# S5 in chunks of four tokens with three tables made on the chip; conditioning pairs inside norms; weight slabs used up one at a time

## The chip, the core and the metric

The kernel runs on one core of one Trainium2 chip, as one program with one launch. The metric is device time in microseconds (us), from the first to the last instruction and the little that lies around them. Five engines work side by side and meet through semaphores: PE multiplies matrices into PSUM, DVE and ACT work on SBUF and PSUM element by element, POOL on SBUF alone, and SP issues most of the transfers. A profile names an instruction by its line in the source, its engine and the tiles that it writes and reads.

## What is computed

The model is a decoder trunk of two layers. It handles 256 prompt tokens (one sequence) and 64 sample tokens (8 sequences of 8), so 320 tokens in all, with a width of 1024. Everything is float32. Cut to what matters here:

```python
for layer in range(2):
    sh1, sc1, g1, sh2, sc2, g2 = split(silu(c) @ ada_w[layer] + ada_b[layer])
    h = rmsnorm(x) * (1 + sc1) + sh1
    m = hgrn2(h)  if layer == 0 else  s5(h)
    x = x + g1 * m
    h = rmsnorm(x) * (1 + sc2) + sh2
    f = swiglu(h) if layer == 0 else  moe_top2_of_8(h)
    x = x + g2 * f
y = rmsnorm(x)

def s5(h):                                # 64 groups of 16 channels, 64 complex states in each group
    lam = exp(a * dt)                     # complex, one for each state
    bu  = B @ h                           # 16 channels -> 64 complex states, for each token
    xs[t] = lam * xs[t-1] + bu[t]
    y   = real(C @ xs) + d * h
    z   = gelu(y)
    return (z @ wa) * sigmoid(z @ wb), xs[last]
```

## The kernel before, in words

Activations lie with channels on partitions: `xT` and `hT` hold 8 blocks (`kt`) of 128 channels by 320 tokens. Each engine has one program, written out by hand as a list of instructions and waits, so the order on an engine is the order of the source. The stages follow one another: conditioning pairs 0 to 3, norm, HGRN2 input products (`head_in`, L556), scores and states, output product (L764), norm, dense SwiGLU (`gate_up`, L779, then the output product at L803), norm, S5, GLU (L870), norm, router, then eight experts (L931) and a last norm.

**Weights** come through `ring`, four slots of one 1 MB slab. SP runs down a fixed list (`slabs`); `put(n)` at L326 waits until `slab_credit` reaches n + 1 and then issues the load. The semaphore starts at 3, and PE adds to it when it begins to use a slab, for by then the slab before it is used up. In the dense output product PE waits for both halves of a block (two slabs of 704 KB), adds one credit at the first product, and the second half's credit only at the start of the conditioning product that follows (`mod_rows(q, half, 5, 2)`). In `gate_up` and GLU two slabs are likewise credited together.

**Conditioning** is made in 24 pairs of slabs, q = 0 to 23. A pair is two `mod_rows` on PE (L499), a copy by ACT (`mod_copy`, L1055), a `mod_turn` on PE (L512) and a `mod_bias` on DVE. Pairs 4 to 11 lie beside the HGRN2 input products, 12 to 15 in the dense output product, 16 to 23 in the S5 stage.

**A norm** is a Square on ACT (L1037), column sums on PE (L535), a Sqrt on ACT (L1040), and a reciprocal, products and shifts on DVE, which end with `h_ready`.

**S5** goes through 16 windows of two state groups (a state group is 128 partitions: two channel groups of 64 states). `states_in` (L825) multiplies all 320 tokens by the real and the imaginary input matrix, ACT copies the result from PSUM (L1140), `rotate` turns it by the angle of the token (the prompt part on POOL at L1702, the sample part on DVE), DVE runs real scans along the tokens with the magnitude as factor (L1527, L1529), `rotate` turns everything back on DVE (12 operations at L1232), and `states_out` (L836) multiplies by the output matrix. The helper `tt` puts nearly all elementwise products on L1232 (DVE) and L1702 (POOL). Before that, in the HGRN2 input stage, DVE builds the input and output matrices (5120 columns), PE transposes them, POOL stores them to memory (`prep`, 2.6 MB) and SP loads them back (`kept`) after HGRN2 has left the space. The load of the HGRN2 sample state (`st0`) is issued by ACT right after the input products and waits for that store, because it takes the same space.

**After S5** SP writes the final states, waits for that (`s5_out`), and then loads the first five expert slabs; four more wait for the fourth norm. DVE waits for `s5_out` too before it clears the router's tiles.

## Time and profile before

| what | us |
|---|---|
| three runs | 2151.43, 2152.88, 2154.42 |
| median | 2152.88 |
| profiled execution, its own time | 2154.64 |
| its span, from the first to the last instruction | 2152.8 |

Share of the span in which an engine is busy: PE 84%, DVE 54%, ACT 35%, POOL 27%. These are averages over stages that have different limits, so the profile is read stage by stage. The page's line of 40 slices already shows it: PE stands at 9 tenths in most slices and at 4 in slices 15 to 19, and in those DVE stands at 9 and the granted PE clock at 5 tenths. Busy time on PE is modelled (a matrix product in float32 appears as two records, a transposition as one), so distances between starts are safer than busy times.

### The profile page before, as it was taken

How to read it: one execution, taken by the hardware profiler on the slowest of the kernel's cores; microseconds unless marked ns; L12 is line 12 of the kernel's file. 1: busy time of each engine (PE TensorE's matmuls, PEld its weight loads, DVE VectorE, ACT ScalarE, POOL GpSimd, SP SyncE). 2: the span in 40 equal slices, each digit the busy share in tenths (PEclk: the TensorE clock that was granted, in tenths of full speed). 3: DMA queues.
4: the chain of work that ended last, by engine and by line, in shares of the span. 5: the costliest groups of instructions: out<-in, count | busy, mean ns of one | idle time of the engine just before them, and what ended most of it. 6: DMA issues, size and time to landing. Idle time of an engine off the chain costs nothing.

```text
span 2152.8 us, 26882 instructions
## 1 busy us (share of the span) xinstructions
PE 1801.6 (84%) x10335; PEld 1395.8 (65%) x10335; DVE 1152.0 (54%) x1464; ACT 744.9 (35%) x789; POOL 578.7 (27%) x284
## 2 busy tenths in 40 slices
PE   3799998699987754444497899999999999999995
PEld 2568875477755531112175797979888888888793
DVE  4413404300000049999713576767676777778675
ACT  1110020011100011111212575757575757667571
POOL 0000212595000024554300132423233332424140
PEclk7799999899998865555597799999999999999997
DMA  5688121633334421111153498989898988888884
GB/s 178 180 289 268 40 78 40 195 117 117 117 107 138 118 86 57 61 59 59 40 174 124 156 314 293 351 273 338 272 326 291 308 303 298 303 298 301 299 305 141
DMA packets 365803, 420.56 MB, mean 195 GB/s; under 512 B 17948, under 2 KB 339757, under 8 KB 365494
## 3 DMA queue, kind: packets, MB, share of 16 engines
q1 hardware_dynamic: 363542, 413.02, 58.2%
q10 hardware_dynamic: 2064, 4.19, 0.7%
q0 software_dynamic: 144, 2.62, 0.3%
q8 instruction: 35, 0.57, 0.1%
q14 instruction: 18, 0.15, 0.0%
HBM read 410.87 MB, written 8.95 MB: 195 GB/s over the span
## 4 chain that ended last, share of the span: by engine, by line
PE 69%; DVE 19%; issue 4%; DMA 3%; ACT 3%; POOL 1%; SPq 0%; DVEq 0%; ACTq 0%; POOLq 0%
PE PS L931 32%; DVE arena L1232 10%; PE PS L779 9%; PE PS L803 5%; PE PS L917 4%; PE PS L870 3%; PE PS L556 3%; DVE exact L1232 2%; PE PS L673 2%; DVE arena L1527 2%; PE PS L764 2%; PE PS L463 2%; PE PS L535 2%; PE PS L1010 2%; DMA ring<-in_ffn_w_out 1%
## 5 line engine op out<-in xcount | busy, mean ns | idle before, releaser
L931 PE MATMUL PS<-exact 128*112 128x256 f32 (+1 forms) x5280 | 770.5, 305 | 26.1 <-DVE exact L1232 24.0
L931 PEld LDWEIGHTS PS<-exact 128*112 128x112 f32 x5280 | 685.2, 175 | 95.1 <-DVE exact L1232 31.9
L1232 DVE TENSOR_TENSOR exact<-arena,exact 128x2048 fp32r<-128x2048 f32 (+1 forms) x162 | 320.7, 1984 | 128.2 <-ACT exact L1171 126.7
L1171 ACT ACTIVATE exact<-arena 128x2048 fp32r<-128x2048 f32 x162 | 309.7, 1913 | 41.6 <-PE PS L931 41.5
L1702 POOL TENSOR_TENSOR arena<-arena 128x512 f32<-128x512 f32 (+4 forms) x128 | 191.3, 1514 | 448.8 <-ACT arena L1140 398.4
L1702 POOL TENSOR_TENSOR exact<-arena,exact 128x1024 fp32r<-128x1024 f32 x56 | 192.1, 3436 | 258.3 <-ACT exact L1171 258.3
L1232 DVE TENSOR_TENSOR arena<-arena 128x128 f32<-128x128 f32 (+7 forms) x399 | 241.4, 657 | 27.5 <-PE PS L616 14.3
L1232 DVE TENSOR_TENSOR exact<-ring,exact 128x2048 fp32r<-128x2048 f32 (+1 forms) x104 | 229.7, 2215 | 49.0 <-ACT exact L1171 48.1
L1702 POOL TENSOR_TENSOR exact<-ring,exact 128x1024 fp32r<-128x1024 f32 x32 | 104.0, 3249 | 495.2 <-ACT exact L1171 495.2
L1171 ACT ACTIVATE exact<-ring 128x2048 fp32r<-128x2048 f32 x104 | 198.0, 1912 | 20.5 <-PE PS L931 20.5
L779 PE MATMUL PS<-hT,ring 128*128 128x320 f32 x704 | 192.2, 436 | 12.8 <-DVE hT L1256 12.8
L779 PEld LDWEIGHTS PS<-hT,ring 128*128 128x128 f32 x704 | 135.1, 192 | 69.9 <-DVE hT L1256 13.3
L836 PE MATMUL PS<-arena 128*32 128x320 f32 x128 | 37.7, 741 | 144.0 <-DVEq L1532 144.0
L803 PE MATMUL PS<-arena,ring 128*128 128x320 f32 x352 | 116.2, 498 | 31.2 <-DMA ring<-in_ffn_w_out 30.2
L803 PEld LDWEIGHTS PS<-arena,ring 128*128 128x128 f32 x352 | 77.4, 223 | 69.8 <-issue 48.6
L1232 DVE TENSOR_TENSOR arena<-arena,PS 112x256 f32<-112x256 f32 (+2 forms) x162 | 78.6, 490 | 79.1 <-PE PS L651 44.9
L836 PEld LDWEIGHTS PS<-arena 128*32 128x32 f32 x128 | 9.2, 158 | 169.3 <-DVEq L1532 158.3
L556 PE MATMUL PS<-hT,ring 128*128 128x320 f32 x384 | 109.7, 443 | 0.8 <-DMA ring<-in_hgrn_w_in 0.8
L1232 DVE TENSOR_TENSOR arena<-work,PS 128x320 f32 x22 | 10.8, 489 | 182.1 <-PE PS L779 182.1
L1232 DVE TENSOR_TENSOR gtmp<-PS,mod 128x64 f32<-128x64 f32 x16 | 3.6, 225 | 177.5 <-PE PS L803 149.7
L556 PEld LDWEIGHTS PS<-hT,ring 128*128 128x128 f32 x384 | 73.5, 195 | 34.0 <-issue 6.8
L463 PE MATMUL PS<-const,arena 112*128 112x112 f32 (+8 forms) x322 | 56.8, 283 | 42.2 <-DVE xT L1330 21.9
(189 smaller groups left out, 1644.1 us busy)
## 6 DMA issues: line engine op xcount, KB each, us to landing
arena<-in_moe_w_in SPq DMA_DIRECT2D x109, 1024.0 KB, 7.5
ring<-in_moe_w_in SPq DMA_DIRECT2D x75, 1024.0 KB, 9.2
arena<-in_moe_w_out SPq DMA_DIRECT2D x56, 1024.0 KB, 5.1
ring<-in_ada_w SPq DMA_DIRECT2D x48, 1024.0 KB, 6.5
ring<-in_moe_w_out SPq DMA_DIRECT2D x33, 1024.0 KB, 7.3
ring<-in_ffn_w_in SPq DMA_DIRECT2D x22, 1024.0 KB, 6.3
ring<-in_hgrn_w_in SPq DMA_DIRECT2D x16, 1024.0 KB, 8.0
ring<-in_ffn_w_out SPq DMA_DIRECT2D x16, 704.0 KB, 4.6
```

Of the source, the lines that this page charges most:

```text
L463: return pe.transpose(out, in_, ident[0:k, 0:k])
L535: last = pe.matmul(PS[:, 7, 0:T], const[:, C_ONE:C_ONE + P], hT[:, k, :], start=(k == 0), stop=(k == KT - 1))
L556: last = pe.matmul(PS[:, bank, 0:T], ring[:, n % RING, k * 256 + (h % 2) * P:k * 256 + (h % 2) * P + P], hT[:, k, :], start=(k == 0), stop ...
L779: last = pe.matmul(PS[:, 2 * (t % 2) + m, 0:T], ring[:, (n + m) % RING, k * 256 + sub * P:k * 256 + sub * P + P], hT[:, k, :], start=(k == ...
L803: last = pe.matmul(PS[:, dt % 2, 0:T], ring[:, (n + k // 11) % RING, (k % 11) * P:(k % 11 + 1) * P], mid[:, k, :], start=(k == 0), stop=(k ...
L836: last = pe.matmul(PS[q:q + 32, 4 + k % 2, 0:T], cct[a][:, k, q:q + 32], vb[w % 2][a][:, j, :], start=(a == 0), stop=(a == 1), skip_group_ ...
L870: last = pe.matmul(PS[:, 2 * sub + m, 0:T], ring[:, (n + m) % RING, k * 256 + sub * P:k * 256 + sub * P + P], hT[:, k, :], start=(k == 0), ...
L917: last = pe.matmul(PS[:, 6 + half, k * P:k * P + CAP], htok[0:TOK[i], i, kk * P:(kk + 1) * P], pick[0:TOK[i], i, :], start=(i == 0), stop= ...
L931: last = pe.matmul(out, a[x], w[y], start=first and m == 0, stop=end and m == 2)
L1171: A(wparts[0][:, j % HRING, :], eslab(j), ACT.Copy).then_inc(sem("rounded"), 1)
L1232: return V.tensor_tensor(out, a, b, op)
L1702: return G.tensor_tensor(out, a, b, op)
```

## The change

**S5** works on chunks of four tokens: 80 chunks (64 of the prompt, two for each sample). PE transposes `hT` for each token of the chunk (`tokens_out`, 4 transpositions for each block), DVE copies, PE transposes again (`chunks_in`, 4 transpositions) so that (token in chunk, channel) lies on partitions, ACT copies to `u2`. One table `Zm` takes the 64 inputs of a chunk to the state that the chunk adds (`states_in`: 16 products of 64 by 64 by 80 for each block). Angles are turned and scanned over 64 chunks only (`turn_and_scan`, four times: three operations of 128x512, two scans of 512 and six operations of 128x504 on DVE, and three of 128x512 on POOL for the other half of the first rotation); samples need no scan, POOL makes their two chunks with ten operations of 128x64. The table `Tm` takes the chunk's inputs to its own outputs and `Cy` takes the state before the chunk to its outputs (`y_out`, 24 products for each block); the result is transposed back (`y_back`, 4 transpositions), and GELU follows block by block. The three tables are made in the HGRN2 input stage as 15 jobs on PE (`gen_jobs`), with powers of lambda on DVE (for B: 24 products and sums of 128x512, ahead of DVE's part in the first job) and on POOL (for C: 24 more of 128x512); they fill 11264 columns instead of 5120, so store and reload are 5.8 MB.

**Conditioning**: pair 16 comes ahead of the third norm, 17 and 18 lie inside it, 19 to 21 in the S5 stage, 22 and 23 in the fourth norm. **Slabs**: every slab gives its own credit. The GLU slabs come ahead of pairs 22 and 23 in the list. **The state load** `st0` moves to behind ACT's fourth value copy (s == 3).

The diff, cut to its core:

```diff
@@ order of slabs
         for q in range(16, 24):
             slabs += [("ada", q, 0), ("ada", q, 1)]
-        slabs += [("glu", j) for j in range(8)]
+            if q == 21:
+                slabs += [("glu", j) for j in range(8)]
+        gen_jobs = [("x0", 0), ("C", 0), ("C", 1), ("C", 2), ("C", 3), ("K", 0), ("K", 1)] + [("Z", m) for m in range(8)]
+        gen_after = {0: range(0, 3), 1: range(3, 5), 3: range(5, 8), 4: range(8, 11), 5: range(11, 13), 6: range(13, 15)}
@@ SP
-                load(cnat[a], I[nm].rearrange("l (k g) c s -> (g c) (l k) s", g=8), "ld_bc")
+                for u in range(2):
+                    load(cnat[a][:, :, 64 * u:64 * u + 64], ...)
...
-            sp.wait_ge(sem("z_ready"), 1)
+            sp.wait_ge(sem("z_ready"), KT)
             for j in range(XRING):
                 if j == NX:
                     sp.wait_ge(sem("h_ready"), 4)
+                    sp.wait_ge(sem("mod_rows_psum"), 24)
                 load_slab(j, 0)
@@ PE
+                if between:
+                    between()
                 pe.wait_ge(sem("h_ready"), norms[0])
...
+            def gen_job(n):
+                kind, m = gen_jobs[n]
+                bank = 6 + n % 2
+                if n >= 2:
+                    pe.wait_ge(sem("gen_dve"), dve_gens(n - 1))
+                    if act_gens(n - 1):
+                        pe.wait_ge(sem("gen_act"), act_gens(n - 1))
...
-                if pair == 3:
-                    pe.wait_ge(sem("mats_made"), 1)
...
+                for n in gen_after.get(pair, ()):
+                    gen_job(n)
...
+                for half in range(2):
+                    n = slab_of["fout", dt, half]
+                    arrived(n)
+                    for k in range(11):
+                        last = pe.matmul(PS[:, dt % 2, 0:T], ring[:, n % RING, k * P:k * P + P], mid[:, half * 11 + k, :], ...)
+                        if k == 0:
+                            last.then_inc(slab_credit, 1)
...
-                mod_rows(q, dt % 2, 5, 2 if dt < KT - 1 else 1)
+                mod_rows(q, dt % 2, 5)
             mod_turn(15, 4)
-            norm()
+            mod_pair(16, 5, 4)
+            def during_norm():
+                mod_pair(17, 5, 4)
+                mod_rows(18, 0, 5)
+                mod_rows(18, 1, 5)
+            norm(during_norm)
...
+            for kt in range(KT + 2):
+                if kt < KT: tokens_out(kt)
+                if 1 <= kt <= KT: chunks_in(kt - 1)
+                if kt >= 2: states_in(kt - 2)
...
+            mod_turn(18, 7)
+            mod_pair(19, 6, 7)
+            mod_pair(20, 6, 7)
+            for kt in range(KT + 1):
+                if kt < KT: y_out(kt)
+                if kt: y_back(kt - 1)
+                if kt == 3: mod_pair(21, 6, 7)
...
+            norm(during_norm)
+            mod_turn(23, 6)
@@ ACT
+                if between:
+                    between()
                 act.wait_ge(sem("sum_psum"), norms[0])
...
-            act.wait_ge(sem("prep_stored"), 16)
+                if s == 3:
+                    act.wait_ge(sem("prep_stored"), 16)
+                    act.dma_start(st0..., I["state_hgrn"]...).then_inc(sem("ld_state"), 16)
...
-            for q in range(12, 16):
+            for q in range(12, 17):
                 mod_copy(q, 5)
...
+            mod_copy(19, 6)
+            mod_copy(20, 6)
+            last_states(0)
+            last_states(1)
+            for kt in range(KT):
+                if kt in (4, 6): last_states(kt // 2)
+                y_taken(kt)
+                if kt == 3: mod_copy(21, 6)
+                if kt >= 2: gelu(kt - 2)
@@ DVE, HGRN2 input stage
...
+            dve.sem_inc(sem("b_powers"), 1)
+            for pair in range(4):
+                if pair:
+                    mod_bias(3 + pair, 4)
+                for n in gen_after.get(pair, ()):
+                    take_gen(n)
@@ DVE, S5
+            def turn_and_scan(q):
+                tt(wi_, im, c, ALU.mult)
+                step(tt(dtmp[0], re, s, ALU.mult))
+                step(tt(wi_, wi_, dtmp[0], ALU.subtract))
+                dve.sem_inc(sem("im_turned"), 1)
+                dve.wait_ge(sem("re_turned"), q + 1)
+                for w in (wi_, wr_):
+                    last = V.tensor_tensor_scan(w, magk[:, 512 * q:512 * q + 512], w, 0.0, ALU.mult, ALU.add)
...
+                tt(xi, xi, t1, ALU.add).then_inc(sem("x_made"), 1)
...
+            for kt in range(KT):
+                tokens_taken(kt)
+            dve.wait_ge(sem("tables_ready"), 1)
+            turn_and_scan(0)
+            turn_and_scan(1)
+            for q in range(18, 21):
+                mod_bias(q, 7)
+            skip_added(0)
+            skip_added(1)
+            turn_and_scan(2)
+            skip_added(2)
+            mod_bias(21, 7)
+            skip_added(3)
+            turn_and_scan(3)
...
+            for kt in range(4, KT):
+                skip_added(kt)
@@ POOL, HGRN2 input stage
+            pool.wait_ge(sem("gen_dve"), 5)
...
+            pool.wait_ge(sem("gen_dve"), 7)
...
+            pool.wait_ge(sem("gen_dve"), dve_gens(len(gen_jobs)))
+            pool.wait_ge(sem("gen_act"), act_gens(len(gen_jobs)))
+            pool.dma_start(prep, made).then_inc(sem("prep_stored"), 16)
@@ POOL, S5, for each of four q
+                tt(w, re[:, :, 0:64], rot_c[:, gs, :], ALU.mult)
+                step(tt(ptmp[0], im[:, :, 0:64], rot_s[:, gs, :], ALU.mult))
+                step(tt(w, w, ptmp[0], ALU.add))
+                pool.sem_inc(sem("re_turned"), 1)
...
+                pool.sem_inc(sem("samples_made"), 1)
```

## Rows read from the trace of the kernel before

**Rows 1.** Busy time by stage: window, length, PE, PEld, DVE, ACT, POOL, PEclk, DMA, GB/s.

```profile
84.00:187.00 103.00, 101.30 (x618) 70.73 (x619) 21.13 (x45) 15.69 (x34) 0.72 (x1) 0.98 0.80 258
...
611.00:768.00 157.00, 126.17 (x501) 83.92 (x504) 7.03 (x27) 1.79 (x3) 0.00 (x0) 0.85 0.42 125
...
790.00:1074.00 284.00, 122.99 (x583) 53.17 (x583) 262.87 (x464) 42.09 (x141) 136.55 (x96) 0.50 0.18 60
...
1204.00:2111.00 907.00, 877.98 (x5974) 774.34 (x5974) 670.94 (x568) 591.96 (x486) 295.76 (x88) 1.00 0.89 302
```

**Rows 2.** Groups by line in the S5 stage: count, busy us, mean ns, idle before.

```profile
L1232 DVE TENSOR_TENSOR arena<-arena 128x512 f32<-128x512 f32 x96 | 96.7, 1061 | 1.1
...
L836 PE MATMUL PS<-arena 128*32 128x320 f32 x128 | 37.7, 741 | 144.0 <-DVEq L1532 144.0
```

**Rows 3.** S5 stage in time order: start us, us, what, count, idle before.

```profile
789.94 2.51 PE L825 MATMUL PS<-hT,arena 32*128 32x320 f32 x8 [9.78 <-DVE hT L1256]
...
796.68 1.94 PE L499 MATMUL PS<-ring,siluc 128*32 128x256 f32 x16
...
838.09 11.31 DVE L1232 TENSOR_TENSOR arena<-arena 128x512 f32<-128x512 f32 x12
...
1056.97 0.67 DVE L1527 TENSOR_TENSOR_SCAN arena<-sT,arena 128x256 f32<-128x256 f32 x1
...
1057.85 5.04 DVE L1232 TENSOR_TENSOR arena<-arena 128x512 f32<-128x512 f32 x12
...
1065.28 1.88 PE L512 MATMUL PS<-const,work 128*128 128x9 f32 x8
```

**Rows 4.** Other rows of the timeline: transpositions cold, DVE and POOL operations alone.

```profile
89.23 1.42 DVE L1232 TENSOR_TENSOR arena<-arena,sT 128x512 f32<-128x512 f32 x2
...
418.36 4.45 POOL L1702 TENSOR_TENSOR arena<-arena,sT 128x512 f32<-128x512 f32 x4
...
1175.68 5.38 PE L463 MATMUL PS<-const,hT 128*128 128x128 f32 x24
```

**Rows 5.** Dense output product, timeline: two blocks and the loads for the second.

```profile
611.64 12.08 PE L803 MATMUL PS<-arena,ring 128*128 128x320 f32 x44 [1.00 <-DVEq L1496]
...
612.86 11.81 SPq L326 DMA_DIRECT2D ring<-in_ffn_w_out  x2
...
623.65 1.07 PE L499 MATMUL PS<-ring,siluc 128*32 128x256 f32 x16
...
628.86 15.11 PE L803 MATMUL PS<-arena,ring 128*128 128x320 f32 x44 [4.14 <-DMA ring<-in_ffn_w_out]
```

**Rows 6.** Third norm, timeline.

```profile
768.46 0.60 ACT L1055 ACTIVATE work<-PS 128x512 f32<-128x512 f32 x1 [40.50 <-PE PS L499]
...
770.53 2.34 ACT L1037 ACTIVATE hT<-xT 128x2560 f32<-128x2560 f32 x1 [1.47 <-DVEq L1506]
...
772.88 1.28 ACT L1040 ACT_TABLE_LOAD   x1
...
772.91 7.25 PE L535 MATMUL PS<-hT,const 128*128 128x320 f32 x16 [2.74 <-ACT hT L1037]
```

**Rows 7.** HGRN2 input and value stage, timeline of PE.

```profile
97.54 8.88 PE L556 MATMUL PS<-hT,ring 128*128 128x320 f32 x32
...
131.94 1.10 PE L463 MATMUL PS<-const,arena 128*128 128x128 f32 x8
...
243.65 4.80 PE L628 MATMUL PS<-arena 128*128 128x8 f32 x32
```

**Rows 8.** DMA issues: what, count, KB, us to landing.

```profile
s_prep<-arena POOLq DMA_DIRECT2D x1, 2560.0 KB, 13.6
...
arena<-in_state_hgrn ACTq DMA_DIRECT2D x1, 0.5 KB, 26.1
```

**Rows 9.** Expert slabs, timeline: the first five loads and the first two roundings.

```profile
1120.88 8.36 SPq L424 DMA_DIRECT2D arena<-in_moe_w_in  x5
...
1183.11 3.69 ACT L1171 ACTIVATE exact<-arena 128x2048 fp32r<-128x2048 f32 x2
```

More of the change, by code:

```diff
@@ L528, in _, with norm @@
             norms = [0]
-            def norm():
+            def norm(between=None):
                 norms[0] += 1
@@ L840, in _, with mod_pair @@
-            NW = GP // 2
-            for w in range(NW):
-                states_in(w)
-                mod_rows(pairs2[w // 2], w % 2, 6)
-                if w:
-                    states_out(w - 1)
-                if w > 1 and w % 2 == 0:
-                    mod_turn(pairs2[w // 2 - 1], 7)
-            states_out(NW - 1)
-            mod_turn(pairs2[-1], 7)
-            pe.wait_ge(sem("mod_ready"), 24)
-            pe.wait_ge(sem("fin_states"), NW)
+            def mod_pair(q, rows, turn):
+                mod_rows(q, 0, rows)
+                mod_rows(q, 1, rows)
+                mod_turn(q, turn)
@@ L1029, in _, with norm @@
             norms = [0]
-            def norm():
+            def norm(between=None):
                 norms[0] += 1
@@ L1395, in _ @@
             step(tt(decp, chunk[:, :, 2], chunk[:, :, 3], ALU.mult))
-            for q in range(8, 12):
-                mod_bias(q, 4)
+            for n in gen_after[4]:
+                take_gen(n)
+            for pair in range(5, 9):
+                mod_bias(3 + pair, 4)
+                for n in gen_after.get(pair, ()):
+                    take_gen(n)
             dve.wait_ge(sem("ld_masks"), 16)
```

664 lines of the change are left out of this document (416 added, 248 removed).

## The prediction

> **What bounds the kernel now.** I read the busy time by stage first, then the groups and the timeline inside each stage that the change touches. In the HGRN2 input stage and in the expert loop PE is busy for 101.3 of 103 us and 878 of 907 us at a granted clock near 1.0: there only work on PE counts, and the loop is left as it is [rows 1]. In the S5 stage PE is busy for 123 of 284 us at half clock, and DVE for 263 of 284 [rows 1]: DVE is the bound, and the output products wait 144 us in total for it [rows 2]. In the dense output product PE is busy for 126 of 157 us while no other engine comes near [rows 1]: something is waited for, and the timeline names a load [rows 5].
>
> **S5 stage: 284 us now.** Prices first. PE is cold there (0.50), and I leave it cold: the turns on DVE leave PE idle for several us each, and after a wait of 4.14 us the dense output product restarted slow [rows 5]. A cold transposition with 128 weight columns is 5.38/24 = 0.224 us [rows 4], so four are 0.9. A product in float32 is two records. If weight columns set the pace, `states_in` with 64 columns is 2 x 0.112 = 0.224 us and 16 are 3.6; if moving columns do, at the rate of the present input products on separate strips of rows (four of 320 columns in 2.51 us, 1.96 ns a column [rows 3]), 80 columns are 0.157 and 16 are 2.5. I take 2.7, near the row on strips, since the two halves lie on separate rows too. `y_out` has 80 weight and 64 moving columns: 24 products are between 3.0 and 6.7 us; here weights are the longer side, so I take 5.5. Weights read with a stride of four tokens occur in no row; at worst they load at a quarter of the rate, 32 x 0.67 = 21 us, at best for nothing more, and I take nothing.
>
> A DVE operation of 128x512 alone is 1.42/2 = 0.71 us [rows 4], a scan of 512 at most 2 x 0.67 = 1.34 [rows 3]. A turn is 9 x 0.71 + 2 x 1.34 = 9.1, with hand-offs 9.5. Beside POOL twelve operations take 11.31 us instead of 5.04 [rows 3], and the mean in the stage is 1.06 [rows 2]; with that factor of 2.24 a turn is 17. I take 9.5, for POOL needs at most 13 operations of 4.45/4 = 1.1 us, 14.5 us for each q [rows 4], and can do q = 0 and 1 while DVE still copies tokens and q = 2 and 3 while DVE waits for `back_psum`.
>
> The chain from `h_ready`: (a) PE's first pass costs 0.9 + 0.9 + 2.7 = 4.5 us a block; the eighth `tokens_out` ends after 0.9 + 1.8 + 5 x 4.5 + 0.9 = 26, say 27 us, and all eight copies stand ahead of the first turn on DVE. (b) A copy and two turns: 20. (c) PE's `mod_turn(19)` needs `mod_bias(18)`, which DVE has queued behind two turns; then 1.88 + 2 x 1.94 + 0.60 + 1.88 and a hand-off [rows 3, 6]: 8.4. (d) DVE's `skip_added(1)` stands ahead of turn 2 and needs the second `y_back`, which PE issues behind the third `y_out`: 3 x 5.5 + 2 x 0.9 = 18.3. (e) Then turn 2 (10.1 with the skip) against PE's `y_out(3)`, `y_back(2)` and pair 21, 12.8: PE is later. (f) `skip_added(3)` needs `y_out(4)` and `y_back(3)`: 7.0. (g) Turn 3: 9.5. (h) Two `y_out`, three `y_back`, copy, skip and GELU (about half a microsecond each): 16. The sum is 27 + 20 + 8.4 + 18.3 + 12.8 + 7.0 + 9.5 + 16 = 119. **-165 us.** Turned from DVE-bound, the stage becomes a chain of hand-offs, in which PE and DVE wait in turn.
>
> **Dense output product.** The load of the second half for the next block is issued only when `mod_rows` begins: the two issues lie at 612.86 and near 624.7, and PE then waits 4.14 us [rows 5]. There are seven such waits (4.1 to 4.5 us, 30 in sum), and after each the 44 records take 14.6 to 15.1 instead of the 12.08 of the first block, for PE restarts at half clock: 7 x 2.8 = 20. With its own credit the load goes out half a block earlier, 6 us, and the wait that it has to cover is 4.1 to 4.5. What is late next is nothing that I see: DMA was busy for 0.42 over 157 us [rows 1], so over 107 it is 0.62. 8 x (12.0 + 1.07) and three `mod_turn` are 107. **-49 us.** `gate_up` and GLU have PE busy throughout, so their credits bring nothing.
>
> **Norms.** Third norm: ACT's Square now stands behind `mod_copy(16)`. PE turns pair 15, then needs two `mod_rows` of 1.07 [rows 5]; Square starts at about +5.7 from the last product instead of +3.2 (770.53 [rows 6]): +2.5. Sqrt stands behind `mod_copy(17)`, which needs two `mod_rows` behind the column sums (1.07 to 1.94 each), a copy of 0.60 and then the table load of 1.28, now hidden under the sums because nothing lies between Square and Sqrt [rows 6]: +4.2 to +6.0. **+8 us.** Everything on DVE waits behind that Sqrt. Fourth norm: the same +4.2 to +6.0, and `mod_turn(23)` (1.88 [rows 3]) ahead of the router: **+7 us.** The Trainium skill (ScalarE: Activation LUTs, What ACT_TABLE_LOAD costs) adds a drain of 1.38 us to each switch of tables; no row here separates one, and by it the two norms would cost 2.8 us more.
>
> **HGRN2 input stage**, all on PE. Removed: four groups of eight transpositions (the first 1.10 us [rows 7]), 5.4 us with their waits. Added: 16 transpositions at 1.10/8 = 0.14 warm [rows 7], 2.2; K, 64 products with two records of half the columns, 0.14 each, 8.8; Z, 128 of the same, 17.6 one by one or 8.8 with both halves side by side, taken at 13. A stall: job 2 waits for DVE's part of job 0, which stands behind eight small operations and 24 of 0.71, so until about 84.2 + 1.6 + 17 + 0.8 = 103.6, while PE is there 97.5 [rows 7] plus 1.1: 5 us, and 3 for the cold restart [rows 5]. The transfers hide in DMA's free fifth [rows 1]. -5.4 + 2.2 + 8.8 + 13 + 8 = **+27 us**, bounds 15 and 38.
>
> **Store and state load**, costed at nothing. 2.6 MB took 13.6 us, so 5.8 MB take 30, and the state load takes 26.1 [rows 8]: 56 us. From the last job (end of pair 6) to the first use (243.65 [rows 7]) lie a pair of 11.5 us (8.88 [rows 7] and its conditioning) and 60 us of values and scores. ACT's own wait at s == 3 comes after 36 us; eight value copies, and PE with them, are queued behind it. The cover is 6 us there and 15 in all; gone, it costs its excess one for one. The reload of 20 us stands ahead of one dense slab on SP, which PE needs 18 us after it starts on the first two: hidden.
>
> **Expert slabs.** SP's final-state stores and the first slabs now stand behind the put for `ada 23`, which needs PE in pair 22: the first load goes out some 20 us behind GLU's last product, not 25 ahead of it (1120.88 [rows 9]). The first rounding was at 1183.11 [rows 9], 37 us behind that product, and comes 7 later; by 907/264 x 0.89 = 3.1 us a slab [rows 1] all nine are in some 28 us after the first issue. Nothing.
>
> **Sum:** -165 - 49 + 8 + 7 + 27 = -172. The profiled execution took 2154.6 us (span 2152.8), 1.8 more than the median shown; 2154.6 - 172 = 1983, and I round to 1984 for hand-offs.
>
> **Rivals.** *Heavier S5*: POOL and DVE meet in every turn (17 us) and halves don't overlap (3.6 and 6.7): 4 x 7.5 + 5 x 0.9 + 7 x 1.2 = 43, so 2027. For it, the present contention; against, POOL runs ahead. *Halves side by side*: products at 2.5 and 3.0, 7 x 2.5 + 1 = 18 less, 1966; for it, the row of 2.51 us; against, `y_out`'s long weights. The Trainium skill (TensorEngine Tiling (Array Packing), Key Properties) lets tiles of the array load and multiply in parallel, which is this rival, but says too that a change of tiling mode drains the array, and S5 changes mode within each block; no row here shows a drain. *Late state load*: at half rate beside the slabs, store and load take 112 of 71 us, +41, 2025. *The slab credits don't do it*: if the wait is the load's own length, the 49 stay, 2033; against, a lead of 6 us for a wait of 4.5. *Slower than before*: the late start leaves the expert loop loader-bound. A slab has 3.44 us; from 4.1 us a slab on (264 x 0.65 = 172) the kernel is slower; at 4.3 it gives 2210. Against: 0.89 busy leaves room, and only nine slabs start late.
>
> **Chances.** Forecast 0.62; heavier 0.14; late state load 0.10; side by side 0.08; credits 0.03; slower 0.02; no change by mishaps that cancel 0.01. The forecast's own bounds (S5 from -20, if PE stayed warm, to +21 for strided weights, the input stage -12 to +11) and two of the heavier cases together give 1940 to 2055. About 0.2% is what a measurement of this kernel can tell from no change; faster 0.97, same 0.01, slower 0.02.
>
> **What would show it.** Right: S5 from `h_ready` to GLU near 119 us with DVE under half busy; no idle between L803's blocks; the Sqrts 6 to 9 us later after their Squares; a PE gap of 5 us in the first pair. Wrong: DVE operations near 1.06 us in the turns; a PE gap near the value copies; the expert loop longer than 907 us.

## The result, and the profile after

The changed kernel takes 1945.6 us (median, 1944.6 to 1946.6) against 2152.2 for the kernel before in the same comparison: a ratio of 0.904, with a 95% interval of 0.903 to 0.906. The forecast was 1984 with 1940 to 2055: the sign is right, the time lies within the range, 6 us from its lower end, and the gain of 207 us is 38 larger than the 169 forecast. The profiled execution has a span of 1944.1 us against 2152.8, so 208.7 us have to be placed.

Busy time by stage, after the change (window, length, PE, PEld, DVE, ACT, POOL, granted clock of PE, share of DMA, GB/s), as [rows 1] of before:

```profile
84.00:201.00 117.00, 112.69 (x972) 82.44 (x971) 29.55 (x59) 20.69 (x45) 34.94 (x39) 0.97 0.69 224
642.00:748.00 106.00, 105.90 (x492) 72.45 (x496) 6.34 (x25) 1.79 (x3) 0.03 (x1) 1.00 0.62 185
773.50:860.50 87.00, 60.45 (x871) 51.89 (x871) 50.73 (x72) 21.81 (x61) 41.19 (x52) 0.74 0.24 76
995.00:1902.00 907.00, 877.83 (x5973) 774.30 (x5973) 671.19 (x568) 591.73 (x486) 295.64 (x88) 1.00 0.89 302
```

S5 fell from 284 to 87 us and DVE in it from 263 to 51 of busy time; the dense output product fell from 157 to 106, all of it PE at a full clock; the expert loop is what it was. The input stage's window grew from 103 to 117 us.

The same marks in both traces, first instruction of each stage in us from the span's start, give the whole account. (The first input product itself starts at 83.70 instead of 85.11, for a group of four transpositions no longer stands ahead of it and `h_ready` comes half a microsecond earlier; this is left in the first row.)

| up to | before | after | shift | this stage's part |
|---|---|---|---|---|
| first value product | 183.95 | 211.61 | +27.7 | +27.7 |
| first dense output product | 611.64 | 642.10 | +30.5 | +2.8 |
| end of the dense output product | 768.40 | 748.85 | -19.6 | -50.0 |
| first work of S5 on PE | 789.94 | 773.58 | -16.4 | +3.2 |
| first GLU product | 1074.0 | 860.4 | -213.6 | -197.2 |
| router | 1165.5 | 956.6 | -209.0 | +4.6 |
| end of the span | 2152.8 | 1944.1 | -208.7 | +0.3 |

The +4.6 is the fourth norm with 5.6 more and GLU with 1.0 less. Of the +2.8, 1.7 are a longer wait of `gate_up` for `h_ready` in the second norm (14.5 us instead of 12.8); no run asks why.

The +27.7 at the first value product is two things. This is the timeline of the changed kernel there (start, duration, engine, line, operation, count, idle before):

```profile
101.81 0.99 PE L462 MATMUL PS<-const,arena 128*128 128x128 f32 x4 [4.06 <-DVE arena L1553]
...
187.20 2.08 PE L573 MATMUL PS<-const,arena 64*64 64x64 f32 x64
...
190.05 23.15 SPq L320 DMA_DIRECT2D ring<-in_hgrn_w_in  x4
190.51 0.56 POOL L1970 DMA_DIRECT2D s_prep<-arena  x1 [37.18 <-ACT arena L1168]
...
211.61 2.90 PE L694 MATMUL PS<-ring,hT 128*128 128x256 f32 x6 [10.86 <-DMA ring<-in_hgrn_w_in]
```

The input stage's own work ends at 200.75, 16.8 us later than before (183.95). Then PE waits 10.86 us for a slab that was asked for at 190.05. Half a microsecond later POOL issues the store of the tables; the list of DMA issues has it with 5632 KB and 19.7 us to landing, where [rows 8] had 2560 KB and 13.6. The slab lands 21.4 us after its issue. The other three loads of that line are issued only at 199.5, 200.3 and 212.8.

The dense output product, as [rows 5]: no idle between two blocks any more, and the second takes as long as the first.

```profile
642.10 12.08 PE L821 MATMUL PS<-arena,ring 128*128 128x320 f32 x44 [0.89 <-DVEq L1684]
...
655.11 12.11 PE L821 MATMUL PS<-arena,ring 128*128 128x320 f32 x44
```

The third norm on ACT, as [rows 6]: the table load, which lay under the column sums, now stands behind a conditioning copy and ahead of the Sqrt.

```profile
753.05 2.33 ACT L1127 ACTIVATE hT<-xT 128x2560 f32<-128x2560 f32 x1
761.93 0.60 ACT L1147 ACTIVATE work<-PS 128x512 f32<-128x512 f32 x1 [6.56 <-PE PS L498]
762.55 1.28 ACT L1132 ACT_TABLE_LOAD   x1
763.84 0.53 ACT L1132 ACTIVATE root<-PS,epst 128x320 f32<-128x320 f32 x1
```

And S5, as [rows 3]: first PE's pass (one block's transpositions and `states_in`), then the marks of the last two `tokens_out`, three turns on DVE and the transpositions behind four output blocks, each line in the order of time within its group.

```profile
773.58 1.94 PE L462 MATMUL PS<-const,hT 128*80 128x128 f32 x8 [6.47 <-DVE hT L1422]
...
779.44 0.44 PE L462 MATMUL PS<-const,arena 80*128 80x80 f32 x4
779.81 1.32 PE L880 MATMUL PS<-arena 64*64 64x80 f32 x32
...
787.46 0.67 PE L462 MATMUL PS<-const,hT 128*80 128x128 f32 x4
```

```profile
788.78 2.08 DVE L1398 TENSOR_TENSOR arena<-arena 128x512 f32<-128x512 f32 x3
...
823.85 4.84 DVE L1398 TENSOR_TENSOR arena<-arena 128x512 f32<-128x512 f32 x3
...
840.85 2.01 DVE L1398 TENSOR_TENSOR arena<-arena 128x512 f32<-128x512 f32 x3
```

```profile
820.37 0.50 PE L462 MATMUL PS<-const,arena 80*128 80x80 f32 x4
822.86 0.50 PE L462 MATMUL PS<-const,arena 80*128 80x80 f32 x4
...
839.56 0.79 PE L462 MATMUL PS<-const,arena 80*128 80x80 f32 x4
844.00 0.80 PE L462 MATMUL PS<-const,arena 80*128 80x80 f32 x4
```

The last group is a clock for `y_out`: between two of these marks lie one block of 24 products and one `y_back`. Early in the stage that is 2.49 - 0.50 = 1.99 us for the block, late 4.44 - 0.79 = 3.65. The granted clock in fine windows explains it:

```profile
773.50:777.00 3.50, 3.42 (x17) 2.86 (x18) 1.50 (x4) 0.44 (x1) 0.00 (x0) 0.50 0.16 50
777.00:782.00 5.00, 5.00 (x87) 4.47 (x86) 1.60 (x3) 2.40 (x6) 0.00 (x0) 0.92 0.02 3
782.00:787.50 5.50, 5.50 (x114) 5.05 (x113) 1.83 (x3) 2.84 (x7) 5.08 (x8) 1.00 0.00 0
...
835.50:840.40 4.90, 4.56 (x53) 4.28 (x54) 0.86 (x4) 0.74 (x3) 0.54 (x1) 0.50 0.01 3
840.40:849.00 8.60, 4.39 (x52) 4.04 (x52) 8.35 (x12) 1.60 (x6) 0.00 (x0) 0.50 0.00 0
849.00:860.50 11.50, 11.13 (x115) 10.02 (x115) 3.23 (x11) 3.15 (x9) 0.00 (x0) 0.50 0.01 1
```

PE enters S5 at half clock (0.50, 1.2 GHz), is at full clock (2.4 GHz) before the first pass is half done, and is back at half for the last 25 us.

### The profile page after: what moved, and what is told of

The parts are those of the page before. It is cut to its first block, busy times and chain, and to the rows that moved or that the text cites. A ratio compares the mean times of both kernels' runs of the same rounds, so it can differ in the third digit from the quotient of the medians.

```text
span 1944.1 us, 27995 instructions
## 1 busy us (share of the span) xinstructions
PE 1748.9 (90%) x11183; PEld 1406.2 (72%) x11183; DVE 951.3 (49%) x1092; ACT 733.9 (38%) x728; POOL 445.6 (23%) x248
## 4 chain that ended last, share of the span: by engine, by line
PE 78%; DVE 11%; issue 5%; ACT 3%; DMA 2%; POOL 1%; SPq 0%; DVEq 0%; ACTq 0%; POOLq 0%
PE PS L1021 35%; PE PS L802 10%; PE PS L821 5%; PE PS L1007 4%; PE PS L954 4%; DVE arena L1398 3%; PE PS L585 3%; DVE exact L1398 2%; PE PS L694 2%; PE PS L462 2%; PE PS L785 2%; PE PS L498 2%; PE PS L1100 2%; ACT exact L1337 2%; PE PS L534 2%
## 5 line engine op out<-in xcount | busy, mean ns | idle before, releaser
L1398 DVE TENSOR_TENSOR exact<-arena,exact 128x2048 fp32r<-128x2048 f32 (+1 forms) x162 | 320.8, 1984 | 128.3 <-ACT exact L1337 127.0
L802 PE MATMUL PS<-hT,ring 128*128 128x320 f32 x704 | 191.8, 436 | 14.5 <-DVE hT L1422 14.5
L1934 POOL TENSOR_TENSOR arena<-arena 128x512 f32<-128x512 f32 (+5 forms) x82 | 88.9, 1106 | 141.3 <-DVE arena L1560 47.5
L821 PE MATMUL PS<-arena,ring 128*128 128x320 f32 x352 | 96.9, 435 | 0.9 <-DVEq L1684 0.9
L462 PE MATMUL PS<-const,arena 112*128 112x112 f32 (+9 forms) x370 | 62.9, 282 | 35.1 <-DVE xT L1496 22.2
L821 PEld LDWEIGHTS PS<-arena,ring 128*128 128x128 f32 x352 | 66.2, 190 | 30.9 <-DVE xT L1398 1.6
L1147 ACT ACTIVATE work<-PS 128x512 f32<-128x512 f32 x24 | 14.4, 599 | 191.9 <-PE PS L498 191.9
L1398 DVE TENSOR_TENSOR arena<-arena 128x512 f32<-128x512 f32 (+9 forms) x131 | 77.2, 623 | 18.3 <-PE PS L637 12.7
L1007 PE MATMUL PS<-arena 128*128 128x112 f32 (+1 forms) x432 | 80.2, 319 | 4.8 <-DVE arena L1849 4.8
L1007 PEld LDWEIGHTS PS<-arena 128*128 128x128 f32 (+1 forms) x432 | 64.2, 202 | 21.5 <-issue 7.8
```

Source lines behind the costliest of these rows:

```text
L462: return pe.transpose(out, in_, ident[0:k, 0:k])
L802: last = pe.matmul(PS[:, 2 * sub + m, 0:T], ring[:, (n + m) % RING, k * 256 + sub * P:k * 256 + sub * P + P], hT[:, k, :], start=(k == 0), ...
L821: last = pe.matmul(PS[:, dt % 2, 0:T], ring[:, n % RING, k * P:k * P + P], mid[:, half * 11 + k, :], start=(half == 0 and k == 0), stop=(h ...
L1007: last = pe.matmul(PS[:, 6 + half, k * P:k * P + CAP], htok[0:TOK[i], i, kk * P:(kk + 1) * P], pick[0:TOK[i], i, :], start=(i == 0), stop= ...
L1398: return V.tensor_tensor(out, a, b, op)
L1934: return G.tensor_tensor(out, a, b, op)
```

## Experiments

All of them start from the changed kernel, but for one that starts from the kernel before. Times are medians; where two kernels are compared, their ratios to the kernel before on the same chip are used (changed kernel: 0.904; 0.001 of it is 2.15 us, and each interval is about 0.002 to either side).

### 1. The dense output product: where do 50 us come from?

`credit2` undoes one part.

```diff
-                for half in range(2):
-                    n = slab_of["fout", dt, half]
-                    arrived(n)
+                n = slab_of["fout", dt, 0]
+                arrived(n)
+                arrived(n + 1)
...
-                mod_rows(q, dt % 2, 5)
+                mod_rows(q, dt % 2, 5, 2)
```

> The changed kernel with one part undone: in the dense output product a block waits for both of its slabs, and the second slab's credit is given only by the conditioning rows behind the block, as before the change. Theory (the single credits carry the whole gain of this stage): seven waits of 4.1 to 4.5 us and slow restarts of 2.5 to 3 us come back, the stage takes 157 us instead of 106, and the kernel 1945.6 + 50 = 1996 us. Rival (the wait was the load's own length, and something else in the change took it away): no more than 5 us longer, 1946 to 1951.

Measured: 2001.9 us, ratio 0.930, so 56 more. That is 6 above the forecast of that run. In its trace the stage is 49.9 us longer. Its waits on PE from 640 to 802 us (waiting tile and line, releaser: us in total, times, longest):

```profile
PE PS L821 <- DMA ring<-in_ffn_w_out: 31.2, 7, 4.6
PE PS L498 <- DMA ring<-in_ada_w: 2.1, 1, 2.1
```

Seven waits, 31 us, and the rest is the half clock behind each, as [rows 5] had it. Some 5 us more fall in the third norm: the conditioning slab of pair 16 comes 2.1 us late, and what PE then does runs at half clock.

`before_credits` makes the same part alone in the kernel before.

```diff
...
-                        last.then_inc(slab_credit, 2 if dt == 0 else 1)
+                for half in range(2):
+                    n = slab_of["fout", dt, half]
+                    arrived(n)
...
+                        if k == 0:
+                            last.then_inc(slab_credit, 2 if dt == 0 and half == 0 else 1)
...
-                mod_rows(q, dt % 2, 5, 2 if dt < KT - 1 else 1)
+                mod_rows(q, dt % 2, 5, 1 if dt < KT - 1 else 0)
```

> The kernel before with one part of the change alone: each half of a dense output block has its own arrival and its own credit. Theory (this part acts by itself, and a full clock at its end also speeds the column sums of the third norm): the stage takes 107 us instead of 157, the sums 4.6 instead of 7.25, and the kernel 50 to 55 us less than before, 2098 to 2104 us. Rival (the load's own length sets the wait): within 10 us of before.

Measured: 2103.8 us, ratio 0.977 (0.975 to 0.979): 50 less, its dense stage without idle. The column sums behind it took 6.69 us, hardly less than 7.25, so the second half of that expectation fell. The part acts by itself and is worth 50 us; "the credits don't do it" is dead.

### 2. The input stage's end: what holds the first value slab?

`store_split` sends the finished part of the tables out early; `store_late` sends all of it later.

```diff
+            pool.dma_start(prep[:, 4096:KEPT], made[:, 4096:KEPT]).then_inc(sem("prep_stored"), 16)
             pool.wait_ge(sem("gen_dve"), dve_gens(len(gen_jobs)))
             pool.wait_ge(sem("gen_act"), act_gens(len(gen_jobs)))
-            pool.dma_start(prep, made).then_inc(sem("prep_stored"), 16)
+            pool.dma_start(prep[:, 0:4096], made[:, 0:4096]).then_inc(sem("prep_stored"), 16)
```

> The changed kernel with the store of the three tables cut in two: the 7168 of 11264 columns that are done first (T, C and the two state terms) go out as soon as T is placed, near 153 us, and only Z's 2 MB at the end of the input stage. Theory (the store of 5.8 MB, issued 0.5 us behind the first value slab, takes the transfers' time from it): PE's wait of 10.9 us ahead of the value products falls to 4 or less, and the kernel takes 1935 to 1941 us. Rival (the slab is late because its own queue gets the credit only at 190 us and four slabs travel together): the wait stays at 9 to 11 us, 1944 to 1947. Second rival (the early store slows the key and query slabs instead): waits of together 4 to 10 us appear between 153 and 190 us, 1945 to 1950.

```diff
+            pool.wait_ge(sem("hin_psum"), 17)
             pool.dma_start(prep, made).then_inc(sem("prep_stored"), 16)
```

> The changed kernel with the store of the three tables issued only after the first value slab's products have begun to end, near 204 us, whole and on the same queue. Theory (the store's 5.8 MB beside four slabs is all that holds the first value slab): PE's wait of 10.9 us ahead of the value products falls to 2 or less, no other wait takes its place because ScalarE asks for the store only near 227 us, and the kernel takes 1934 to 1938 us. Rival (the store collides with the next value slabs or is still under way when ScalarE waits for it): waits of 5 to 10 us between 205 and 245 us, 1942 to 1947 us.

Measured: split 1942.7 us (0.903), late 1932.2 us (0.897). The waits of `store_split` on PE, and then the start of the value products and the store in `store_late`:

```profile
PE PS L498 <- DMA ring<-in_ada_w: 2.9, 2, 1.9
...
PE PS L694 <- DMA ring<-in_hgrn_w_in: 2.2, 1, 2.2
```

```profile
199.43 1.93 PE L498 MATMUL PS<-ring,siluc 128*32 128x256 f32 x32
201.30 3.72 PE L694 MATMUL PS<-ring,hT 128*128 128x256 f32 x16
...
205.61 0.56 POOL L1971 DMA_DIRECT2D s_prep<-arena  x1 [51.72 <-PE PS L694]
```

With the early part gone the wait falls from 10.9 to 2.2, but 2.9 us come back as waits for conditioning slabs, between 171 and 175 us (the early part is issued at 156.4 and lands 12.6 us later): theory and second rival of that run were half right. In the trace the value products start 5.7 us earlier against the first input product; the whole time is 3 us shorter, give or take 5, so no gain is shown, where I had asked for 4 to 10. With the store behind the slab the wait is gone altogether, the value products start 10.9 us earlier against the first input product, and nothing new is waited for: the slab was asked for at the same moment (190.67) and lands 8.2 us later instead of 21.4. So the store was the cause. The two ratios differ by 15 us, give or take 5, and the time is 2 us below the forecast of that run; the spans differ by 9.5. These three agree: 10.9 lies within the interval, and the execution with the trace was the slowest of its four (1936.4 us against 1931.7 to 1932.5). In it the column sums of the second norm took 4.57 instead of 6.26 us, those of the third 7.61 instead of 4.57.

### 3. The two norms: the copy ahead of the Sqrt

```diff
...
-            norm(during_norm)
+            norm()
+            mod_copy(17, 5)
             mod_copy(18, 5)
```

and the same for copy 22 in the fourth norm (ACT's order only).

> The changed kernel with ScalarE's two conditioning copies (17 and 22) behind the Sqrt of their norm instead of ahead of it. Theory (the copy holds the table load and the Sqrt back): the table load goes under the column sums, each Sqrt starts about 0.3 us behind them and 3 to 4 us earlier, and the kernel takes 1937 to 1940 us. Rival (PE's later conditioning rows become what S5 and the router wait for): the Sqrts come earlier but the first transposition of S5 and the router don't, 1944 to 1947.

Measured: 1937.5 us, ratio 0.900, 8 less, give or take 5. ACT in the third norm of `copy_late`:

```profile
751.64 2.33 ACT L1127 ACTIVATE hT<-xT 128x2560 f32<-128x2560 f32 x1
753.99 1.28 ACT L1132 ACT_TABLE_LOAD   x1
758.64 0.53 ACT L1132 ACTIVATE root<-PS,epst 128x320 f32<-128x320 f32 x1 [3.36 <-PE PS L534]
```

From Square to Sqrt it is 7.0 us instead of 10.8. Against the first input product, S5 begins 4.3 us earlier. GLU begins only 3.1 earlier, since S5 is 1.2 longer there: the granted clock is 0.57 from 772 to 777 us and the first block of `states_in` takes 2.40 us instead of 1.44. From GLU's first product to the router it is 5.1 less. The mechanism that the forecast gave for both norms is shown.

### 4. Small products side by side

`same_rows` lets the second product of each pair read rows 0 to 63 as the first does (the second half of the state is left out), so in Z and `states_in` the two share rows but not columns, and in `y_out`, whose outputs lie on partitions 0 to 79 in both cases, they share both.

```diff
...
-                                last = pe.matmul(PS[r, 2 * a + kt % 2, i * NCH:(i + 1) * NCH], Zm[r, gp, a, :], u2[r, gp, :],
+                                last = pe.matmul(PS[r, 2 * a + kt % 2, i * NCH:(i + 1) * NCH], Zm[0:64, gp, a, :], u2[0:64, gp, :],
...
-                        r = slice(64 * u, 64 * u + 64)
+                        r = slice(0, 64)
                         o = PS[0:NCH, (4 if kt % 2 == 0 else 2) + u, 64 * i:64 * i + 64]
```

> The changed kernel, but the second product of each pair (Z, states_in, y_out) reads rows 0 to 63 as the first one does, instead of rows 64 to 127; the second half of the state is left out of the result. Number and shapes of the products stay. Theory (the two products of a pair run side by side because they lie on separate rows): Z's 256 records take 16 to 17 us instead of 8.4, states_in 2.6 us a block instead of 1.32, y_out 3.4 instead of 1.7 where the clock is full and 6 to 7 instead of 3.7 where it is half; S5 grows by 20 to 30 us, the input stage by 8, the kernel takes 1973 to 1985 us. Rival (each product takes its own time whatever rows it reads, and only the clock made the stage shorter than forecast): 1944 to 1949 us.

`same_tile` lets Z and `states_in` share both rows and columns (`PS[0:64, ...]` too); there is one execution of it.

> The changed kernel, but the second product of each pair of Z and of states_in reads rows 0 to 63 and writes partitions 0 to 63 as the first one does; the second half of the state is left out, and the routing that follows from the wrong result may need more passes of the expert loop, so the two stages are read, not the whole time. Theory (two small products run side by side unless they share both rows and columns of the array): Z takes 15 to 18 us instead of 8.4, states_in 2.0 to 2.7 us a block instead of 1.32. Rival (Z and states_in were never side by side, a product of this size is that short): 8.4 and 1.32 stay.

The whole times, 2878.6 and 2877.6 us, hold a second pass of the expert loop (907 us), since the routing follows from the altered result; only the stages are read. In `same_rows`: PE's group of Z in the input stage (line, shapes, count, busy us, mean ns, idle before), then one block of `states_in` and two marks behind output blocks at half clock:

```profile
L573 PE MATMUL PS<-const,arena 64*64 64x64 f32 x256 | 8.4, 220 | 0.0
```

```profile
781.66 1.32 PE L880 MATMUL PS<-arena 64*64 64x80 f32 x32
...
829.64 0.79 PE L462 MATMUL PS<-const,arena 80*128 80x80 f32 x4
836.96 0.79 PE L462 MATMUL PS<-const,arena 80*128 80x80 f32 x4
```

In `same_tile`: two jobs of Z, one block of `states_in`, and the window around it:

```profile
192.54 3.94 PE L573 MATMUL PS<-const,arena 64*64 64x64 f32 x64
...
795.00 4.53 PE L880 MATMUL PS<-arena 64*64 64x80 f32 x32
```

```profile
790.00:810.00 20.00, 20.00 (x137) 18.76 (x136) 2.06 (x3) 3.61 (x9) 10.32 (x16) 0.50 0.00 1
```

Sharing rows alone costs nothing: Z stays at 8.4 us and `states_in` at 1.32, against my expectation. Sharing rows and columns costs the overlap: two jobs of Z go from 2.08 to 3.94 us at full clock, an output block from 3.65 to 7.32 - 0.79 = 6.53 at half. So the products of a pair do run side by side, unless they need the same part of the array. The Trainium skill (TensorEngine Tiling (Array Packing), Key Properties) says that tiles work independently, each tied to its partitions. The trace agrees, with these numbers. The Trainium skill (TensorEngine Tiling (Array Packing), Key Properties) also says that a change of tiling mode drains the array. In the changed kernel's trace a `states_in` product starts at 779.81, when the transposition ahead of it, on 80 rows and 128 columns, is modelled to end at 779.88: no drain of a size that matters here is seen, though a modelled end can't exclude a short one.

The second thing in `same_tile` was not expected: with its products one at a time, `states_in` takes 4.53 us instead of 1.32, more than the overlap explains, because the granted clock stays at 0.50 all through the first pass, though PE has no idle time in it from 790 us on. Only part of the factor of 3.4 is the overlap; a factor of two is the clock.

### 5. The clock in S5's late part

`filler` adds products that nobody reads where PE waits for turns 2 and 3.

```diff
                 if kt == 3:
                     mod_pair(21, 6, 7)
+                for _ in range({3: 10, 5: 8}.get(kt, 0)):
+                    pe.matmul(PS[:, 6, 0:T], ident, const[:, 0:T], start=True, stop=True)
```

> The changed kernel with 18 products added on TensorE that nobody reads: 10 behind pair 21 and 8 behind y_back(4), where TensorE waits for turns 2 and 3. Theory (the late output products of S5 take 3.7 us a block instead of 1.8 only because the clock is granted at half after these waits): y_out(4) to y_out(7) take about 2 us each, S5 becomes 5 to 7 us shorter, 1938 to 1941 us. Rival (the products that fill do not change the clock that y_out gets, or are themselves late): y_out stays at 3.7, 1945 to 1950 us.

Measured: 1940.5 us, ratio 0.900 (0.899 to 0.902), 8 less by the ratio, give or take 5; in the traces S5 is 3.7 us shorter. Windows of `filler`, to hold beside those of the changed kernel above:

```profile
835.50:840.40 4.90, 3.99 (x83) 3.49 (x83) 2.82 (x6) 1.01 (x3) 1.45 (x2) 1.00 0.02 3
840.40:849.00 8.60, 6.57 (x65) 4.88 (x62) 8.21 (x17) 1.33 (x5) 0.00 (x0) 1.00 0.00 0
849.00:860.50 11.50, 11.35 (x107) 9.35 (x104) 2.32 (x6) 5.09 (x11) 0.00 (x0) 0.55 0.04 5
```

`y_out(4)` and `y_out(5)` now run at full clock. The second filling ends at 846.1, two microseconds ahead of `y_out(6)`, and from 851 us on the granted clock is 0.50 again, so the last two blocks gain little. The mechanism holds; in S5 it brought 3.7 us where I expected 5 to 7.

### 6. The order of S5, and all together

`s5_order`: ACT's last states ahead of copies 19 and 20, turn 2 ahead of the first skips on DVE, pairs 19 to 21 behind `y_out(3)`, `y_out(5)` and `y_out(6)` on PE.

```diff
             mod_turn(18, 7)
-            mod_pair(19, 6, 7)
-            mod_pair(20, 6, 7)
...
+            mod_bias(18, 7)
+            turn_and_scan(2)
             skip_added(0)
             skip_added(1)
-            turn_and_scan(2)
+            turn_and_scan(3)
...
```

> The changed kernel with three things of S5 in another order: ScalarE keeps the last states of the first two quarters before, not behind, conditioning copies 19 and 20; VectorE does turn 2 before the skips of blocks 0 and 1; conditioning pairs 19, 20 and 21 stand behind y_out(3), y_out(5) and y_out(6) on TensorE instead of ahead of y_out(0) and behind y_out(3). Theory (the stage is a chain of hand-offs that goes through the pairs and skips because of the order on the engines): the idle stretch of VectorE between turn 1 and turn 2 (809 to 824 us) closes, S5 takes 68 to 74 us instead of 86.8, the kernel 1928 to 1935 us. Rival (GpSimd's half of the turns and its share of the memory port set the pace, turns become longer as they follow each other): turns of 13 us or more, S5 80 to 87, 1940 to 1946 us.

Measured: 1940.4 us, ratio 0.900; S5 takes 81.4 us, 5.4 less. Turn 2 begins at 814.1 instead of 823.9 and all turns are done at 836 instead of 849, as the theory had it, but PE does not follow. Its windows:

```profile
809.00:820.00 11.00, 9.94 (x118) 9.40 (x119) 10.75 (x12) 4.19 (x14) 9.30 (x10) 0.50 0.01 1
820.00:830.00 10.00, 6.88 (x75) 4.45 (x72) 9.79 (x12) 1.25 (x4) 9.32 (x10) 0.50 0.12 31
830.00:840.00 10.00, 9.28 (x105) 8.81 (x102) 7.26 (x11) 2.17 (x7) 6.32 (x8) 0.50 0.55 181
```

Without the pairs ahead of it, `y_out` starts at half clock at 803 us, and all three windows up to 840 have 0.50; PE becomes the late one. Both numbers lie in the rival's ranges, but not for its reason: the turns take 10 to 11 us, not 13 or more. Neither theory foresaw the clock.

`best` puts this order, the split store and the late copies together.

> The changed kernel with three edits together: the store in two parts, the copies 17 and 22 behind their Sqrt, and S5's new order. If the three act on separate parts of the path, the savings add: about 3 (store, measured) + 8 (copies, measured) + 11 to 18 (order), 1917 to 1924 us. Rival (the store's part comes back later as it did in part before, and the order's part is smaller because pairs then meet the shorter norm): 1925 to 1935 us.

Measured: 1919.7 us, ratio 0.892 (0.890 to 0.894), in the range for savings that add. That range counted 11 to 18 us for the order, which alone gave 8 by the ratio and 5.4 in S5's length. By their ratios the three parts alone add up to 19 us, and together they give 26, give or take 6; that alone would not show an excess. In the trace S5 takes 76.9 us, 9.9 less than in the changed kernel, and the granted clock is 1.00 from 820 us on, where `s5_order` has 0.50 up to 840. So in these traces the order is worth more beside the other two edits than alone; what raised the clock there, no run shows.

`best2` takes the late store, the late copies, a second order (skips 0 and 2 and two conditioning biases inside turns 2 and 3, pairs cut up into PE's waits) and 18 products that nobody reads; `best2_nofill` is the same without these 18.

```diff
             mod_turn(18, 7)
-            mod_pair(19, 6, 7)
-            mod_pair(20, 6, 7)
+            fill(8, 6)
+            rows_of(19)
...
+                if kt == 4:
+                    pe.wait_ge(sem("y_read"), 3)
+                    fill(4, 4)
...
+                if kt == 5:
+                    mod_turn(21, 7)
+                    fill(6, 6)
...
```

> The changed kernel with the late store, the copies 17 and 22 behind their Sqrt, and a second order of S5: skips 0 and 2 and two conditioning biases inside turns 2 and 3, the conditioning pairs 19 to 21 taken apart into TensorE's waits, and 18 products that nobody reads in three of these waits. Theory (the first new order was bound by TensorE at half clock behind 809 us; with the waits filled the clock stays at full and y_out takes 1.8 us a block): S5 takes 66 to 72 us, the kernel 1903 to 1911 us. Rival (the filling work comes too late or pushes the pairs onto the path): S5 stays at 76 to 80 us, 1912 to 1920 us.

> The last kernel without its 18 products that nobody reads; the late store, the copies behind their Sqrt and the second order of S5 stay. Theory (the clock that the filled waits keep is what made the second order shorter than the first): y_out falls back to about 3.7 us a block in part of the stage, S5 takes 75 to 79 us instead of 69.6, the kernel 1913 to 1918 us. Rival (the order alone did it, the pairs in TensorE's waits are filling enough): S5 stays at 69 to 72 us, 1905 to 1910 us.

Measured: 1907.2 us (ratio 0.886, 0.883 to 0.888) with S5 at 69.6 us, and 1912.9 us (0.888, 0.886 to 0.890) with S5 at 75.5. Windows of the late part, first with the filling work, then without:

```profile
809.00:820.00 11.00, 8.64 (x123) 7.45 (x123) 10.75 (x15) 2.45 (x8) 8.69 (x12) 1.00 0.43 139
820.00:830.00 10.00, 8.47 (x124) 6.87 (x123) 4.75 (x14) 5.53 (x14) 0.00 (x0) 1.00 0.01 2
```

```profile
809.00:820.00 11.00, 9.86 (x113) 9.46 (x114) 10.75 (x17) 2.34 (x8) 3.81 (x6) 0.59 0.40 129
820.00:830.00 10.00, 9.98 (x111) 9.31 (x112) 3.01 (x12) 3.17 (x10) 0.00 (x0) 0.50 0.01 2
```

In the traces the 18 products are worth 5.9 us of S5, and the clock is what they change; the whole times differ by 6 us, give or take 7. `best2` is the fastest version seen: 0.886 of before, some 40 us below the changed kernel by the ratio.

## Why the prediction was right, and where it was not

The sign, the stages that gain and the links of the chain were right. The sum was not: S5 came out 32 us below its forecast, the norms 7 and the input stage 10 below theirs, and the store cost 11 that stood at nothing. That the time lies within the range is in part luck: S5 alone is 12 us beyond its own bound of -20, and with the store out of the way (`store_late`, 1932.2 us) the time is below the range. Of the signs named beforehand, the blocks of the dense output product without idle time came, and the gap of 5 us in the first pair (4.06). Three did not: S5 took 87 us and not 119, DVE was busy for 58% of it and not under half, and the Sqrt came 3.2 us later against the last dense product in the third norm and 3.8 later against its Square in the fourth, not 6 to 9. And one sign of being wrong came, a gap of PE near the value copies, though not by the state load that it stood for.

**S5, -165 forecast, -197 measured.** The chain was the right one: the stage became hand-offs between PE and DVE, DVE busy for 51 of 87 us, and each link is in the trace. Their lengths, forecast and measured: (a) 27 and 14.5, (b) 20 and 21.0, (c) 8.4 and 7.5, (d) 18.3 and 6.8, (e) 12.8 and 12.4, (f) 7.0 and 4.6, (g) 9.5 and 8.8, (h) 16 and 11.2; together 119 and 86.8. The work of DVE was priced well: turn 3, which has DVE to itself, takes 8.4, and three operations of 128x512 in it 2.01.

What failed is the premise under the prices of PE, "PE is cold there", that is at half clock. It was reasoned from the old stage, where PE waits for DVE all the time; the new first pass has no such waits, and the clock rose 3.5 us after it began. So (a) is a term of the right work at half the price: 2.7 for `states_in` would be about right at half clock (twice 1.32), and 0.9 for four transpositions was 0.67 and 0.44. In (d) the same: PE comes there from two conditioning pairs and runs `y_out` at 1.99 us a block.

In (f) and (h) PE was cold as forecast, and there the other choice was off: `y_out` at 5.5, near the bound for products one by one (6.7; measured 6.5), where side by side it is 3.65. The rival "halves side by side" was true as a mechanism, but its 18 us were priced at half clock, as the forecast's own `y_out` was. A warm PE stood only among the bounds, for 20 us, and no case had both at once.

Weights read with a stride of four tokens (`tokens_out`), priced at nothing with 21 us at worst, cost nothing that shows: four of these transpositions take 0.67 us at full clock, for 128 moving columns; the four of `chunks_in`, on weights without a stride, take 0.44 for 80, about as much a column. In link (e) the order was the reverse of the forecast: turn 2 is the late one (beside POOL its first three operations take 4.84 us instead of 2.01), and PE waits 6.4 us for it. The contention that "heavier S5" lived on is there, but only in part of turns 0 to 2.

**Dense output product, -49 forecast, -50.0 measured,** and shown by undoing it and by doing it alone. Six microseconds of lead were enough for a wait of 4.5.

**Norms, +8 and +7 forecast, +3.2 and +4.6 measured** (the second with GLU, which is 1.0 shorter). Square and Sqrt come late for the reasons given, which `copy_late` shows; the order of copy and Sqrt is 4 to 5 us of each norm. The third norm's miss is mostly the column sums, 4.57 us here instead of the 7.25 of [rows 6], where PE had been idle for 2.74 us ahead of them. The changed kernel and its versions have pair 16 and 1.16 or 1.17 us of idle time there in eleven traces; nine show 4.57 or 4.58, but `store_late` 7.61 and `same_tile` 7.58. So most executions gain these 3 us, not every one. The Trainium skill (ScalarE: Activation LUTs, What ACT_TABLE_LOAD costs) adds a drain of 1.38 us to each switch of tables. Here the copy ends at 762.53, the load starts at 762.55 and takes 1.28, and the Sqrt starts at 763.84, so there is no room for one, and the measurement decides.

**HGRN2 input stage, +27 forecast, +16.8 measured.** K took 7.7 (8.8 forecast), Z 8.4 (13): Z was taken between one by one and side by side, and it is wholly side by side. The stall behind the powers of lambda was 4.06 (5), the restart after it 1.3 rather than 3.

**Store, nothing forecast, +10.9 measured.** This is the step that was wrong in kind. The forecast asked whether store and state load would be done in time for who waits for them, and that held: ACT asks for the state at 238.1, when the store has landed 28 us ago, and no product waits for the state. Its prices for the two were too high: 30 us for the store, which took 19.7, and 26.1 for the state load, which took 18.7. It did not ask what a store of 5.8 MB does to the transfers beside it; "The transfers hide in DMA's free fifth" is a statement on a mean over the stage, and behind 190 us the store and the slabs together had DMA busy to the full (a share of 1.10 from 190 to 200 us and 0.97 from 200 to 212). The two misses in the input stage, -10 and +11, cancelled; a sum that comes out right says nothing on its terms.

**The rest at nothing** held: the expert loop takes 907 us as before, and its first product comes 38.5 us behind the router in both traces.

## What to carry to other kernels

Price a stage that is rebuilt by the work that will surround its instructions, not by the clock of the stage that it replaces: state which engine will wait there, and give the price at both levels of PE's clock. A transfer that nobody waits for still has a price, paid by the load beside it; look for the next load that a bound engine needs, and issue the store behind it. Where an engine's order puts a copy between a Square and its Sqrt, or a conditioning pair ahead of a hand-off, moving it costs one line and gave 8 us here, give or take 5.

## What the runs showed of the hardware that was not expected

- Two products of 64 rows that read the same rows and write different columns run side by side as well as two on separate rows (1.32 us a block of `states_in` either way), and two on separate rows that write the same partitions in different banks do too (`y_out`, 3.65 against 6.53 us). Only with both in common do they follow one another.
- With `states_in` one product at a time the granted clock stayed at 0.50 in every window from 776 to 830 us, 40 of them with PE busy throughout; with the products in pairs it was 0.92 after 3.5 us and then 1.00.
- The column sums of the third norm, behind the same work and the same 1.2 us of idle time, took 4.57 us at a granted clock of 1.00 in the changed kernel's trace and 7.61 at 0.59 in that of `store_late`. Nine of eleven traces show the short time. So 3 us of a norm in one trace can be the clock of that execution.
